# Two transformer models in one launch on one core: the leading two weight blocks behind six norms multiplied side by side, weight splits and conditioning turns placed elsewhere, and the output sent in four transfers

## The reference

```python
h = modulate(rms_norm(x, norm1_g[i]), sh1, sc1)
a_z, bq, bk, bv, cq, ck, cv = split_proj(h @ w_in[i])
...
x = x + g1 * (jnp.concatenate([out_a, out_b, out_c], axis=-1) @ w_out[i])
x = x + g2 * conv_ffn(modulate(rms_norm(x, norm2_g[i]), sh2, sc2),
                      w_up[i], conv_w[i], conv_b[i], w_down[i])
```

## Time and profile before

| | |
|---|---|
| time, median of 3 runs | 1632.85 us (1630.95 to 1634.07) |
| the profiled execution | 1631.75 us |
| its span | 1629.6 us |
| mean granted TensorE clock | 0.982 of full |
| PE busy | 1553.1 us, 95% of the span |
| DVE busy | 1054.8 us, 65% |
| ACT busy | 842.1 us, 52% |
| POOL busy | 98.4 us, 6% |
| DMA | 287.47 MB, 176 GB/s |

### The profile page before, as it was taken

One profiled execution on the slowest core, in us unless ns is written; L12 is line 12 of the kernel. 1 busy time (PEld: TensorE's weight loads), 2 busy tenths in 40 slices (PEclk: granted clock), 3 DMA queues, 4 the chain that ended last, 5 costly groups with the idle time before them and its releaser, 6 DMA issues.

```text
span 1629.6 us, 27723 instructions
## 1 busy us (share of the span) xinstructions
PE 1553.1 (95%) x9546; PEld 1279.1 (78%) x9546; DVE 1054.8 (65%) x1819; ACT 842.1 (52%) x1517; POOL 98.4 (6%) x152
## 2 busy tenths in 40 slices
PE   4999989899999999899899999999999999799997
PEld 2777667688888888697779998697788887578886
DVE  4443874756555477666678876654568865778864
ACT  4442872544444223455656655536566654567653
POOL 0121000000000111020000000030100001000000
PEclk9999999999999999899999999999999999799999
DMA  9765106232232587342167658442856678636663
GB/s 377 275 217 186 40 1 248 76 97 96 91 102 84 184 274 245 111 146 86 51 231 270 182 184 319 144 130 104 334 222 186 181 275 294 238 116 186 179 179 113
DMA packets 77152, 287.47 MB, mean 176 GB/s; under 512 B 9057, under 2 KB 12641, under 8 KB 67089
## 3 DMA queue, kind: packets, MB, share of 16 engines
q1 hardware_dynamic: 61120, 190.23, 36.6%
q0 software_dynamic: 15952, 96.18, 15.8%
HBM read 282.44 MB, written 1.05 MB: 174 GB/s over the span
## 4 chain that ended last, share of the span: by engine, by line
PE 86%; DVE 5%; DMA 4%; ACT 2%; issue 2%; SPq 0%; DVEq 0%; ACTq 0%
PE B L1816 16%; PE B L1799 15%; PE B L1800 15%; PE B L1801 15%; PE B L1814 8%; PE B L1836 3%; PE B L2059 2%; DMA MW<-in_wmod 2%; DMA RAW<-in_wup 1%; PE B L1828 1%; PE B L1830 1%; PE B L1829 1%; DVE NORM L1267 1%; PE B L2113 1%; PE B L1981 1%
## 5 line engine op out<-in xcount | busy, mean ns | idle before, releaser
L1145 DVE TENSOR_TENSOR WLO<-RAW,WHI 128x1024 fp32r<-128x1024 f32 (+1 forms) x376 | 412.3, 1099 | 172.1 <-ACT WHI L700 171.9
L700 ACT ACTIVATE WHI<-RAW 128x1024 fp32r<-128x1024 f32 (+1 forms) x376 | 358.7, 958 | 175.5 <-PE B L1801 98.5
L1799 PE MATMUL B<-HHL,WHI 128*128 128x256 f32 (+1 forms) x1168 | 397.9, 341 | 19.2 <-DVE HHL L1251 12.5
L1801 PE MATMUL B<-HHL,WLO 128*128 128x256 f32 (+1 forms) x1168 | 390.8, 335 | 0.0
L1800 PE MATMUL B<-HHL,WHI 128*128 128x256 f32 (+1 forms) x1168 | 390.7, 335 | 0.0
L1799 PEld LDWEIGHTS B<-HHL,WHI 128*128 128x128 f32 x1168 | 223.7, 192 | 57.8 <-issue 22.3
L1816 PE MATMUL B<-HHL,WHI 128*128 128x512 f32 x704 | 244.6, 400 | 2.1 <-DVE HHL L1251 1.8
L1801 PEld LDWEIGHTS B<-HHL,WLO 128*128 128x128 f32 x1168 | 224.0, 192 | 21.7
L1800 PEld LDWEIGHTS B<-HHL,WHI 128*128 128x128 f32 x1168 | 224.2, 192 | 19.9
L1814 PE MATMUL B<-HHL,WLO 128*128 128x256 f32 x704 | 183.8, 282 | 0.0
L1816 PE MATMUL B<-MID,WHI 128*128 128x512 f32 x462 | 162.4, 399 | 0.0
(11 more groups left out here) (237 smaller groups left out, 2159.6 us busy)
## 6 DMA issues: line engine op xcount, KB each, us to landing
RAW<-in_wup SPq DMA_DIRECT2D x176, 512.0 KB, 3.6
GWR<-in_wmod POOLq DMA_DIRECT2D x33, 1024.0 KB, 8.5
RAW<-in_wdn SPq DMA_DIRECT2D x64, 384.0 KB, 3.5
RAW<-in_wproj SPq DMA_DIRECT2D x44, 512.0 KB, 4.4
RAW<-in_wdn SPq DMA_DIRECT2D x64, 320.0 KB, 3.5
GWA<-in_wmod POOLq DMA_DIRECT2D x19, 1024.0 KB, 5.7
WINV<-in_wmod POOLq DMA_DIRECT2D x32, 512.0 KB, 5.6
RAW<-in_wout SPq DMA_DIRECT2D x24, 512.0 KB, 3.6
```

Of the source, the lines that this page charges most:

```text
L700: act_f(WH[s][:, 0:kts, :], RAW[s][:, 0:kts, :], ACT.Copy).then_inc(hi_done, 1)
L1145: v.tensor_tensor(WL[s][:, 0:kts, :], RAW[s][:, 0:kts, :], WH[s][:, 0:kts, :].bitcast(F32), ALU.subtract).then_inc(lo_done, 1)
L1799: mm(bank[:, 0:t], wh, a, start=first and k == ks[0], stop=False)
L1801: ins = mm(bank[:, 0:t], wl, a, start=False, stop=stop and k == ks[-1])
```

## The change

Five things are edited.

1. A function `pair` on PE takes the leading two weight blocks piece by piece in turn, block 0 into bank 0 and block 1 into bank 1, behind (1, n1), (2, n1) and the four (l, n2). It waits for the splits of both blocks before its first product. For that the first body of the `w_up` loop is written out before the loop (peeled). In layer 2 the projection behind the pair is taken in two halves around the slot that the second block had.
2. DVE issues `lo(kt - 1)` after scaling piece `kt`.
3. In layers 0 and 1 the splits at m = 4 and 5 of `w_out` leave those places: the first goes to m = 6, ahead of ACT's square and behind DVE's accumulation, the second into norm (l, n2), on ACT behind the root, on DVE between the reciprocal and the wait for the spread.
4. Conditioning turn 10 leaves the sums of (3, n1) and stands behind its spread and four units, on DVE in the pooling mixer. Turn 11 moves from c = 2 to c = 0 in (3, n2), and units 4 and 5 of group 11 move from the spread of (3, p1), the norm behind the pooling mixer, to the mixer's blocks 0 and 1.
5. The output goes in four transfers of 128 x 2 x 256.

```diff
-            for kt in range(KT):
-                sp.wait_ge(resid, 8 * 3 + kt + 1)
-                sp.dma_start(A["out"][:, 256 * kt:256 * kt + 256], X[:, kt, 0:256]).then_inc(stored, 16)
+            for c in range(KT // 2):
+                sp.wait_ge(resid, 8 * 3 + 2 * c + 2)
+                sp.dma_start(A["out"][:, 512 * c:512 * c + 512].rearrange("p (k t) -> p k t", k=2),
+                             X[:, 2 * c:2 * c + 2, 0:256]).then_inc(stored, 16)
...
@@ ACT, norms
-                        if c == 2 and key in TURNED:
+                        if key in TURNED and c == {8: 2, 11: 0}.get(TURNED[key]):
                             row_out(TURNED[key])
                 if key != (0, "n1"):
                     roots(key)
+                if key == (3, "n1"):
+                    row_out(10)
+                if IS_L[key[0]] and key[1] == "n2":
+                    ahead(OUT0[key[0]] + 5)
...
@@ ACT, w_out
-                    if m < 6:
+                    if not IS_L[l] and m < 6 or m < 4:
                         ahead(n)
+                    elif IS_L[l] and m == 6:
+                        ahead(n - 2)
...
@@ DVE, norms
-            def roots(r, nt):
+            def roots(r, nt, split=None):
                 dve.wait_ge(rs_ready, r + 1)
                 v.reciprocal(RR[:, 0:nt], RS[:, 0:nt]).then_inc(rr_ready, 1)
+                if split is not None:
+                    ahead(split)
                 dve.wait_ge(rb_ready, r + 1)
...
-                    if kt >= 2 and not (key == (0, "n1") and kt in (4, 5)):
-                        lo(kt - 2)
-                lo(KT - 2)
+                    if kt and not (key == (0, "n1") and kt == 4):
+                        lo(kt - 1)
                 lo(KT - 1)
...
@@ DVE, pooling mixer
                 pool_lo(3)
+                mod_apply(10, 1)
+                derive(3, 2)
...
@@ PE, norms
+                if key == (3, "n1"):
+                    mod_turn(10)
...
-                           (3, "p1"): (11, [4, 5, 6, 7])}
+                           (3, "p1"): (11, [6, 7])}
...
@@ PE, w_up
+                def pair():
+                    for s in range(2):
+                        pe.wait_ge(lo_done, UP0[l] + s + 1)
+                        pe.wait_ge(drained, TUP0[l] + s - 3)
+                    for k in range(KT):
+                        for s in range(2):
+                            how = dict(first=k == 0, stop=k == KT - 1, ks=[k], ready=(nl_ready, nbase))
+                            ins = products_apart(s, 8, banks[s], **how) if wide_up(l) else \
+                                products(s, 8, banks[s], t, **how)
+                            if k == KT - 1:
+                                ins.then_inc(blk_used, 1)
...
-                loop(pe, FT // 2, body)
+                loop(pe, FT // 2, body, peel=True)
...
@@ PE, pooling mixer
+                        if b < 2:
+                            mod_unit(11, 4 + b)
```

More of the change, by code:

```diff
@@ L1206, in norm @@
                 if r:
-                    roots(r, t // P)
+                    roots(r, t // P, OUT0[l] + 5 if IS_L[l] and which == "n2" else None)
                 if key == (3, "n1"):
@@ L1258, in norm @@
                         if kt:
-                            lo(2)
                             lo(3)
@@ L1545, in w_out @@
                         accumulate(l, "out", m - 1, (m - 1) % 2)
+                    if IS_L[l] and m == 6:
+                        ahead(OUT0[l] + 4)
                 if NOUT[l]:
@@ L1802, in products, with products_apart @@
                 return ins
-            def products_apart(s, kts, bank, k0=0, T=HHL, first=True, stop=True, ready=None):
-                for k in range(kts):
+            def products_apart(s, kts, bank, k0=0, T=HHL, first=True, stop=True, ready=None, ks=None):
+                for k in ks or range(kts):
                     if ready:
@@ L2015, in gated_mix @@
                     ins.then_inc(amix, 1)
-                for i in range(NSLOT[l]):
-                    if (2 if l == 0 else 0) <= i < TPROJ[l] - IS_L[l]:
-                        T = TILES[l][i]
-                        n, bank = BASE[l] + T["b"], tile_bank(l, i)
+                def pair():
+                    for b in range(2):
+                        pe.wait_ge(lo_done, BASE[l] + b + 1)
+                    for k in range(KT):
+                        for b in range(2):
+                            ins = products(b, 8, banks[b], proj_tokens(l, names[b] if l == 2 else f"au{b}"),
+                                           first=k == 0, stop=k == 7, ks=[k], ready=(nl_ready, base) if b == 0 else None)
+                            if k == 7:
+                                ins.then_inc(blk_used, 1)
+                for i in range(NSLOT[l]):
+                    if i == 0 and l:
+                        pair()
+                    if 2 <= i < TPROJ[l] - IS_L[l] or l == 2 and i == 1:
+                        tile = 2 if l == 2 and i == 1 else i
+                        T = TILES[l][tile]
+                        n, bank = BASE[l] + T["b"], tile_bank(l, tile)
                         pe.wait_ge(lo_done, n + T["blocks"])
@@ L2026, in proj @@
                         if T["qs"] is None:
-                            ins = products(n % 4, 8, bank, proj_tokens(l, T["name"]),
-                                           ready=(nl_ready, base) if i == 0 else None)
+                            half = l == 2 and i < 3
+                            ins = products(n % 4, 8, bank, proj_tokens(l, T["name"]), first=not half or i == 1,
+                                           stop=not half or i == 2, ks=range(4 * i - 4, 4 * i) if half else None)
                         else:
                             ins = products_tok(n % 4, T["blocks"], bank, T["qs"])
-                        if T["last"]:
+                        if l == 2 and i == 1:
+                            pass
+                        elif T["last"]:
                             ins.then_inc(blk_used, T["blocks"])
```

25 lines of the change are left out of this document (14 added, 11 removed).

## The result

The changed kernel takes 1621.7 us (median of 4 runs, 1620.89 to 1623.06), beside it the kernel before 1631.9 (4 runs, 1629.38 to 1634.07): a ratio of 0.9937 with an interval of 0.9918 to 0.9955, 10.2 us less. Timed a second time, eight runs of it have a median of 1623.9 (1618.20 to 1626.80) beside 1631.62 (12 runs): 0.9954 (0.9936 to 0.9972). 1619.5 was forecast; both medians lie in the range of 1612.5 to 1627, and the gain is 8 to 10 us where 13.3 had been summed.

The account below looks back on a forecast made before the run. PE was taken as the bound, busy 1553.1 of 1629.6 us, so gains come from its idle time. Terms summed to 13.3 off 1631.75, giving 1618.5; 1.1 for the runs' median made 1619.5, range 1612.5 to 1627.

Parts of the forecast that it names:

- (0, n2): Layer 0, norm ahead of `w_up`: pair ends soon after the last low part, less delays; 3.2 us gained.
- w_up(2): Layer 2's `w_up`, behind its second norm: a load pushed behind conditioning fetches lands late; 2.0 us lost, bounds 0 and 4.
- (2, n1): Layer 2's first norm: pair ends 4.5 us sooner, less 0.9 for waits at sums; 3.6 us gained, bounds 2.5 to 4.5.
- the wait ahead of (1, n2): Layer 1, end of `w_out`: with the splits moved away the norm's sums start sooner; 2.2 us taken, up to 2.3.
- (1, n1): Layer 1's first norm: weight splits, not PE, set when the next tile starts; 1.3 us gained.
- the clock in (1, n2): Conditioning units behind the shorter wait may no longer run at 0.50; 1.1 us taken, from 0 to 1.2.
- layer 3: Moved turns and units, the pair behind (3, n2) and shorter mixer waits; 3.7 us gained, bounds 2.4 to 5.5.
- B: Rival: loads run into conditioning weights at more places, both `w_up` losing 4 us; 1626.7 us, chance 0.10.
- C: Rival: pairs hide little because ACT and DVE bound the next work, splits taking PE's place; 1624.5 us, chance 0.13.
- D: Rival: denser PE work keeps the clock up behind the norms, 5 us in all; 1614.5 us, chance 0.13.
- E: Rival: layer 2's late `w_up` load never catches up, 16.8 us lost; slower at 1634.3 us, chance 0.03.
- F: Rival: nothing gained in the norms, only splits, turns and output count; 1630.5 us, chance 0.03.

Follow-up runs that it names:

- lag two: Changed kernel with DVE again issuing a piece's low part two pieces behind the scaling, as before the change; 1620.56 us, one run.
- the pairs alone: Kernel before with only `pair` in its places and layer 2's split projection, nothing else of the change; 1627.39 us, one run.
- changed kernel again: The changed kernel itself, unaltered, timed and profiled a second time; 1623.9 us, median of 8 runs.

## Why the prediction was right, and where its sizes were off

**Right by mechanism and size.** (0, n2): 3.2 forecast, 3.2 measured. The split ahead of the scaling costs 0.8 (1.0 forecast). Lag one brings the last low part 0.6 us later (0.7 forecast), but the pair then ends 1.8 us behind it (1.4 forecast) where with lag two it ends 2.7 behind; on balance lag one gains 0.3. `w_up(2)`: 2.0 and 1.9 lost, by the mechanism named: the load behind the pair lands in 9.1 us (9.3 forecast), and the loss goes when the fetches are spread. Output: 0.4 and 0.4; the pairs alone, with eight transfers, have nothing there.

**Right in sum by luck, (2, n1).** 3.6 forecast, 3.8 measured, but neither of its two terms is right. The pair was to end 4.5 us sooner; it ends 3.8 sooner (15.90 us behind the spread in place of 19.68), since the last low part comes 0.7 later (0.4 forecast) and the pair ends 1.85 behind it (1.4 forecast). And 0.9 was taken off for PE's waits at the sums behind it, of which there are none:

```profile
1044.60 0.95 PE L1994 MATMUL B<-CST,SQ 128*128 128x1 f32 x8
```

**Right in size, half right in mechanism, the wait ahead of (1, n2).** 2.2 forecast and 2.44 measured (3.98 - 1.54). The forecast took the split's own time on ACT and DVE. The pairs alone, with the splits in place, show the wait 1.3 us shorter when the load came sooner: what stood in the way was, for 1.3 us at least, ACT's wait for that load, 3.86 us in the row that the forecast quotes, and moving the split took it out of the squares' way. In layer 0, without such a wait, the same move freed nothing. So that the split's own 2.3 us and the measured 2.44 agree is mostly luck.

**Mis-sized, (1, n1).** That the splits bind in PE's place was right (wait of 1.45). 1.3 was forecast; 1.2 is what it gives where the clock spares it, and -0.8 where it doesn't. The sum had no term for the clock: products behind a wait, and the spread itself, may run at 0.50.

**Mis-sized, the clock in (1, n2).** "behind a wait of 1.8 they may not" run at 0.50: 1.1 us were taken for it. With a wait of 1.54 they did, in both profiles of the changed kernel. In six of the other kernels with that wait they didn't, and from the end of `w_out` into `w_up` 3.5 us were gained there, in place of 2.4. It should have been a bound, not a term.

**Wrong, layer 3.** 3.7 forecast, 1.2 in the first profile, its steps 1.5, -0.3, -0.5, 0.5, and 1.4 in the second. The turn out of (3, n1) gave more than thought (1.5 for 0.8). The order ahead of (3, n2) was to give 1.0 and reads as a loss, since the last sums ran at 0.50 (3.57 us for 16, timeline) where before they ran at full clock. With the half clock through most of the way the old order took 13.0 (pairs alone, 9.5 of it at 0.50) and the new 12.5 (changed kernel again, all of it at 0.50): the order gains 0.5 or more, by one profile of each. The term of 0.7 for the mixer's shorter waits measured -0.3 in one profile and 2.0 in the other, by where the low clock fell. And ahead of the spread behind the mixer PE waits for a reciprocal behind two splits on DVE, 2.0 us, in a row that stood in the trace before.

**The rivals.** B is what `w_up(2)` has, at one place only. C (splits bind) is real at (1, n1) and behind no other pair. D has the right object. The ledger shows the clock taking at single places, but over the runs the mean granted clock is 0.977 to 0.982 in the kernel before (12 runs, 0.980 on average) and 0.982 to 0.985 in the changed one (8 runs, 0.983). An estimate from these: if PE were busy in all of the low stretches, they would cost 0.020 x 1632 = 33 us before and 0.017 x 1624 = 28 now, so that up to 5 of the 7.7 us between these medians may be the clock's. Whether the shorter waits bring that is not shown. E did not come: the loads catch up after 1.9 us. F is ruled out by the pairs alone, which gain 3.7 and 3.1 at the two clearest places.

Forecast 13.3, ledger 8.7 in the first profile, 10.9 in the second. In the first, (1, n1) and (1, n2) lack 2.8 and layer 3 lacks 2.5; in the second, layer 3 lacks 2.3 and the step behind (1, n2) 1.1. The range had room for errors of this size: anything from 5 to 19 us faster would have lain in it.

## What to carry to other kernels

Pairing the first two blocks behind a norm is worth block 1's time only up to the next thing that is late; look at once for the splits and loads that the later release of block 0 pushes back, and behind whose transfers they then stand. A split moved off one chain lands on another: in layer 1 it freed 2.4 us, where the split had waited for a late load with the squares behind it; in layer 0 the same edit cost 0.8. And a sum of small terms should carry no term for a clock that a single profile shows: the same program had it in other places in the next.

## What the runs showed of the hardware that was not expected

The granted clock falls to 0.50, 1.2 of 2.4 GHz, at places that differ between two profiles of one program, by 2 us for one place (1.5 of them by 17 against 29 matmuls in a stretch of 3.3 to 3.4 us). It stayed at 0.50 through 26.9 us in which PE was busy 23.11. A low stretch that begins at a norm's spread delays the first product behind it, which came 4.13 and 4.15 us behind the spread of (1, n1) in two profiles with such a stretch, and 3.56 to 3.58 in six without. In every profile the low stretches stand around norms, the pooling mixer, the start and the end, where PE waits, and never inside the long loops.

A load of 512 KB on SP's queue takes 3.6 us when it is issued ahead of POOL's fetches and 9.1 when it is issued 1.3 us behind the first of four fetches of 1 MB on POOL's queue. By the Trainium skill (DMA: Bandwidth & Descriptors, Rules for kernel authors) transfers from different issuing engines run on the same 16 DMA engines and interleave. The trace agrees: it shares with them and isn't served ahead.
